# One output projection of a decoder trunk: six of eight column pairs as seven block products with GpSimd's sums, and the order of work at two borders of the attention heads

## The reference, cut to what matters

```python
def pool_mixer(h, prefix, qpos, w_in, w_grp, pool_scale, w_out):   # layer 0
    u, z = split(h @ w_in)
    pooled = windowed means of u, less u, in four groups
    y = (pooled per group @ w_grp) * pool_scale * silu(z)
    return y @ w_out            # 2048 x 2048: the projection of this case
x = x + gate(c) * mixer(rms_norm(x) * (1 + scale(c)) + shift(c))
# then shared K and V from x (w_kv), layer 1: attention in three branches with
# proj = h @ w_in_b, y = sum of gate * branch * silu(z), x + gate * (y @ w_out_b)
```

## Time and profile before

| | us |
|---|---|
| median of 3 runs | 2412.46 (2411.96 to 2413.54) |
| the profiled execution's own time | 2413.57 |
| its span, first to last instruction | 2411.8 |
| mean granted TensorE clock | 0.993 of full speed |
| first output projection, eight pairs, TensorE | 724.5 to 909.1 |
| 24 block pairs of the second input projection | to 1723 |
| heads, 8 turns | 1726 to 2120 |

### The profile page before, as it was taken

How to read it: one execution, slowest core, us unless ns; L and a number is a source line. 1 busy time by engine, 2 the same in 40 slices (tenths; PEclk the granted TensorE clock), 3 DMA queues, 4 the chain that set the end, 5 groups by cost and what they waited for, 6 DMA issues and landing times.

```text
span 2411.8 us, 48917 instructions
## 1 busy us (share of the span) xinstructions
PE 2351.8 (98%) x20327; PEld 2217.5 (92%) x20327; DVE 1178.2 (49%) x2057; ACT 824.4 (34%) x1383; POOL 348.4 (14%) x509
## 2 busy tenths in 40 slices
PE   7999999999999999999989999999999999998997
PEld 7988988888899999999989999999989988867997
DVE  1236111222163344333587777777566666654343
ACT  1125121111242233111364444444455455532222
POOL 2002000592000000110110000000032333313000
PEclk9999999999999999999999999999999999999999
DMA  9985887676644435773434444444533333497222
GB/s 341 347 294 189 272 251 246 198 226 225 218 135 146 130 110 190 227 246 108 139 92 132 132 131 131 132 131 132 158 108 104 97 97 105 158 337 281 88 88 89
DMA packets 400917, 419.69 MB, mean 174 GB/s; under 512 B 21734, under 2 KB 353766, under 8 KB 398322
## 3 DMA queue, kind: packets, MB, share of 16 engines
q1 hardware_dynamic: 384610, 349.70, 46.0%
q0 software_dynamic: 16112, 67.14, 8.2%
HBM read 383.59 MB, written 55.27 MB: 182 GB/s over the span
## 4 chain that ended last, share of the span: by engine, by line
PE 92%; DVE 4%; ACT 1%; issue 1%; DMA 1%; POOL 0%; SPq 0%; ACTq 0%; DVEq 0%; POOLq 0%
PE acc L2463 43%; PE acc L2614 19%; PE acc L2641 8%; PE work L2378 4%; PE work L2667 3%; PE work L2318 3%; PE out_acc L2704 2%; PE work L2733 1%; PE acc L2318 1%; PE acc L2689 1%; PE work L2366 1%; PE acc L2746 1%; PE out_acc L2699 1%; PE work L2658 1%; PE work L2549 1%
## 5 line engine op out<-in xcount | busy, mean ns | idle before, releaser
L2463 PE MATMUL acc<-h_hi,w_hi 128*128 128x260 f32 x2832 | 581.6, 287 | 2.5 <-DVE w_lo L1568 1.9
L1568 DVE TENSOR_TENSOR w_lo<-raw,w_hi 128x1024 fp32r<-128x1024 f32 (+1 forms) x220 | 272.4, 1239 | 624.3 <-ACT w_hi L1139 624.2
L2463 PE MATMUL acc<-h_hi,w_lo 128*128 128x260 f32 x2832 | 570.7, 283 | 0.0
L2463 PE MATMUL acc<-h_lo,w_hi 128*128 128x260 f32 x2832 | 569.8, 283 | 0.0
L1139 ACT ACTIVATE w_hi<-raw 128x1024 fp32r<-128x1024 f32 (+1 forms) x220 | 231.0, 1051 | 784.9 <-PE acc L2463 773.5
L2463 PEld LDWEIGHTS acc<-h_hi,w_hi 128*128 128x128 f32 x2832 | 436.0, 189 | 29.1 <-issue 27.7
L2463 PEld LDWEIGHTS acc<-h_hi,w_lo 128*128 128x128 f32 x2832 | 436.8, 189 | 0.0
L2463 PEld LDWEIGHTS acc<-h_lo,w_hi 128*128 128x128 f32 x2832 | 436.7, 189 | 0.0
L1901 DVE TENSOR_TENSOR block_lo<-block,block_hi 128x1024 fp32r<-128x1024 f32 x168 | 205.3, 1223 | 107.0 <-ACT block_hi L1381 106.9
L1381 ACT ACTIVATE block_hi<-block 128x1024 fp32r<-128x1024 f32 x168 | 177.6, 1057 | 191.1 <-DVE block L1936 64.4
L2614 PE MATMUL acc<-t_hi,block_hi 128*128 128x260 f32 x768 | 217.3, 283 | 3.5 <-DVE block_lo L1901 2.1
(11 more groups left out here) (415 smaller groups left out, 3485.5 us busy)
## 6 DMA issues: line engine op xcount, KB each, us to landing
ada<-in_w_ada SPq DMA_DIRECT2D x192, 512.0 KB, 4.8
block<-in_w_in_b SPq DMA_DIRECT2D x96, 512.0 KB, 4.6
raw<-in_w_in_a SPq DMA_DIRECT2D x64, 512.0 KB, 5.0
raw<-in_w_kv SPq DMA_DIRECT2D x48, 512.0 KB, 3.6
raw<-in_w_out_a SPq DMA_DIRECT2D x32, 512.0 KB, 3.8
raw<-in_w_in_b SPq DMA_DIRECT2D x32, 512.0 KB, 4.4
raw<-in_w_out_b SPq DMA_DIRECT2D x32, 512.0 KB, 3.6
pages_early<-in_cache_k_cmp SPq DMA_DIRECT2D x32, 256.0 KB, 4.2
```

The source lines that it names most:

```text
L1568: V.tensor_tensor(LO[j % 2][:, :, 0:n], RAW[j][:, :, 0:n], HI[j % 2][:, :, 0:n].bitcast(F32), ALU.subtract).then_inc(lo_ready, 1)
L2463: last = mm_(out[half][0:n, 0:HT], part[slot][:, kk, cols_], src[:, k, half * HT:(half + 1) * HT], start=(first and part is HI and src is ...
```

## The change

Pairs 0 and 7 of the output projection stay dense. Pairs 1 to 6 become seven block products each: `A_ROLE` says which of the four weight buffers a product takes, A11, A22, A12 or A21 (roles 0 to 3), or a sum that replaced it. GpSimd makes four weight sums of 128 x 1024 in each pair and, during pair 0, four activation sums of 128 x 2080 in place in Y; these are split to TH_A and TL_A by ScalarE (`t_hi_a`) and VectorE (`t_lo_a`). A product is multiplied with its high weights first (16 matmuls) and waits for the low weights only then (8 matmuls). ScalarE copies products 1 and 5 out of PSUM, VectorE reads the others (`a_out`) and adds the rows to X (`row_add`: its last operations, of 8 columns, are the sample tokens'). P7 is added by TensorE into the bank of P6 after VectorE has read that. The squares of the next norm follow the new order of rows. GpSimd's DMAs of the bias table stand between the weight sums.

In the heads, the very first scores come behind the first three pieces instead of ahead of them. `z_out` is cut in two: `z_first` (silu of the first half, which is in SBUF) signals VectorE by `csr`, and in the last turn it stands ahead of the last `turned`; `z_rest` follows. VectorE's product with the first half's z waits for `csr` and no more for the banks.

```diff
-Q_U, ..., Q_OA, Q_KV, Q_G, Q_P, Q_H, Q_OB = 0, ..., 18, 26, 38, 39, 81, 89
+Q_U, ..., Q_OA, Q_KV, Q_G, Q_P, Q_H, Q_OB = 0, ..., 18, 32, 44, 45, 87, 95
+A_PAIR, A_PROD = 6, 7
+A_P1, A_P4, A_P2, A_P5, A_P6, A_P7, A_P3 = range(A_PROD)
+A_ROLE = (0, 1, 2, 3, 3, 0, 2)
...
+        TH_A = nc.alloc_sbuf_tensor_at("y_t_hi", [P, KT, T], F32R, offset=c_at)
+        TL_A = nc.alloc_sbuf_tensor_at("y_t_lo", [P, KT, T], F32R, offset=y_at)
...
# SyncE
-            quads(Q_OA, w_oa, 8)
+            quads(Q_OA, w_oa, 1)
+            def a_load(i, role):
+                k0, c0 = ((0, 0), (8, P), (8, 0), (0, P))[role]
...
+            def a_free(i, role):
+                last = A_PROD * (i - 2)
+                if i == 1:
+                    sp.wait_ge(lo_ready, 4 * Q_OA + role + 1)
+                elif role == 1:
+                    sp.wait_ge(s_sum, 4 * (i - 2) + 3)
+                elif role == 3:
+                    sp.wait_ge(s_sum, 4 * (i - 2) + 4)
+                    sp.wait_ge(lo_ready, a_count(last + A_P6))
+                else:
+                    sp.wait_ge(lo_ready, a_count(last + (A_P7 if role == 0 else A_P3)))
+            for i in range(1, A_PAIR + 1):
+                for role in range(4) if i == 1 else (1, 3, 0, 2):
+                    a_free(i, role)
+                    a_load(i, role)
...
# GpSimd, behind the loads of x
+            b11, b12 = Y[:, 0:8, 0:HT], Y[:, 0:8, HT:T]
+            b21, b22 = Y[:, 8:KT, 0:HT], Y[:, 8:KT, HT:T]
+            pool.wait_ge(ys, 8)
+            nc.gpsimd.tensor_tensor(b11, b12, b11, ALU.subtract).then_inc(s_pooled, 1)
+            pool.wait_ge(ys, KT)
+            nc.gpsimd.tensor_tensor(b12, b22, b12, ALU.subtract).then_inc(s_pooled, 1)
+            pool.wait_ge(s_pooled, 6)
+            nc.gpsimd.tensor_tensor(b22, b22, b11, ALU.subtract).then_inc(s_pooled, 1)
+            pool.wait_ge(s_pooled, 7)
+            nc.gpsimd.tensor_tensor(b21, b22, b21, ALU.subtract).then_inc(s_pooled, 1)
...
+            for i in range(A_PAIR):
+                p = A_PROD * i
+                pool.wait_ge(raw_full[3], 16 * (Q_OA + i + 2))
+                pool.wait_ge(lo_ready, a_count(p + A_P1))
+                nc.gpsimd.tensor_tensor(a11, a11, a21, ALU.subtract).then_inc(s_sum, 1)
+                pool.wait_ge(s_sum, 4 * i + 1)
+                pool.wait_ge(raw_full[1], 16 * (Q_OA + i + 2))
+                nc.gpsimd.tensor_tensor(a21, a21, a22, ALU.add).then_inc(s_sum, 1)
+                if i < NH // 4:
+                    bias_table(i)
+                pool.wait_ge(lo_ready, a_count(p + A_P5))
+                nc.gpsimd.tensor_tensor(a21, a22, a11, ALU.subtract).then_inc(s_sum, 1)
+                pool.wait_ge(s_sum, 4 * i + 3)
+                pool.wait_ge(lo_ready, a_count(p + A_P2))
+                nc.gpsimd.tensor_tensor(a12, a12, a21, ALU.subtract).then_inc(s_sum, 1)
...
# ScalarE
+            hi(Q_OA, 1)
+            t_hi_a(0)
+            hi(Q_OA, 2)
+            t_hi_a(1)
+            t_hi_a(2)
+            hi(Q_OA, 3)
+            t_hi_a(3)
+            a_hi(0)
+            for p in range(A_PROD * A_PAIR):
...
+                    a_hi(p + 1)
...
+                if s in (A_P1, A_P5):
+                    act.wait_ge(w_used, a_count(p))
...
+                    nc.scalar.activation(copy[:, :], bank[:, 0:HT], ACT.Copy).then_inc(st_copied, 1)
+                if s in (A_P4, A_P5):
+                    square_a(2 * i + (s == A_P5))
...
                 if last_turn:
                     turned(i, 6)
+                    z_first(i)
                     turned(i, 7)
-                z_out(i)
+                else:
+                    z_first(i)
+                z_rest(i)
...
# VectorE
+            turn_a(0, {1: lambda: None, 2: lambda: t_lo_a(1), 3: lambda: t_lo_a(0), 0: lambda: (a_lo(0), t_lo_a(3))})
+            for p in range(A_PROD * A_PAIR):
...
+                    a_lo(p + 1)
...
+                if p == 0:
+                    t_lo_a(2)
+                if s in (A_P2, A_P6, A_P7, A_P3):
+                    a_out(p)
+                if s in (A_P4, A_P5):
+                    square_sum_a(2 * i + (s == A_P5))
...
+            def a_out(p):
...
+                elif s == A_P7:
+                    V.tensor_tensor(P1A[:, :], D[3][:, 0:HT], P1A[:, :], ALU.add).then_inc(st_added, 1)
+                    o(V.tensor_tensor(P5A[:, :], P5A[:, :], P1A[:, :], ALU.add))
+                    V.scalar_tensor_tensor(out=P1A[:, :], in0=D[2][:, 0:HT], scalar=-1.0, in1=P1A[:, :],
...
+                    row_add(row + 1, 1, P5A)
+                    row_add(row + 1, 0, P1A).then_inc(s_ute, 1)
+                elif s == A_P3:
+                    V.tensor_tensor(U2A[:, :], D[1][:, 0:HT], U2A[:, :], ALU.add).then_inc(st_added, 1)
...
+                    row_add(row, 1, U2A).then_inc(s_ute, 1)
...
-                if br == 2:
+                if br == 2 and hh == 0:
+                    dve.wait_ge(csr, 18 + i - back + 1)
+                elif br == 2:
                     dve.wait_ge(acc_free, 2 * (D_H + i - back) + 2)
...
# TensorE
-            pairs(Q_OA, D_OA, 8, (ys, 0))
+            for j in range(4):
+                quad(Q_OA, D_OA, j, (ys, 0))
+            def a_product(p):
...
+                elif s == A_P7:
+                    pe.wait_ge(st_added, 5 * i + 2)
...
+                out = D[(0, 2, 0, 1, 3, 3, 1)[s]]
+                k0, at = ((0, 0), (8, 0), (8, 0), (0, 0), (8, HT), (0, HT), (8, HT))[s]
+                b_hi, b_lo = (HH, HL) if s in (A_P1, A_P2, A_P3) else (TH_A, TL_A)
...
+                pe.wait_ge(hi_ready, a_count(p))
+                for kk in range(8):
+                    for part, b in enumerate((b_hi, b_lo)):
+                        mm_(out[:, 0:HT], w_hi[:, kk, :], b[:, k0 + kk, at:at + HT], ...)
+                pe.wait_ge(lo_ready, a_count(p))
+                for kk in range(8):
+                    last = mm_(out[:, 0:HT], w_lo[:, kk, :], b_hi[:, k0 + kk, at:at + HT], ...)
+                last.then_inc(w_used, a_step(p))
+            for p in range(A_PROD * A_PAIR):
+                a_product(p)
+            pe.wait_ge(st_added, A_ADD)
+            for j in range(4):
+                quad(Q_A7, D_A7, j)
...
-                    if u < 6:
+                    if u < 6 and n:
                         scores(n)
                     for at in range(steps[u], steps[u + 1]):
                         piece(i, at)
+                    if n == 0:
+                        scores(n)
```

More of the change, by code:

```diff
@@ L398, in build @@
         GD = place("gates_sample", [P, NBR])
+        RT = [place(f"resid_tmp{i}", [P, TS]) for i in range(2)]
+        assert c_at + KT * T * 4 + 2 * T * 4 <= cursor[0] - 64
         GF = nc.alloc_sbuf_tensor_at("gates_T", [48, T], F32, offset=keep_end - TS * NKV * NCMP * 4)
@@ L1322, in kv_hi @@
+            def kv_hi(k):
+                act.wait_ge(w_used, 4 * Q_A7 + k // 4 + 1)
+                if k < 14:
+                    act.wait_ge(s_ute, 4 + 2 * A_PAIR)
+                else:
+                    act.wait_ge(acc_free, 2 * D_A7 + k - 13)
                 nc.scalar.activation(HH[:, k, :], X[:, k, :], ACT.Copy, scale=vec(2, k)).then_inc(hhi_ready, 1)
-            hi(Q_OA + 7, 1)
-            squares(1, 6)
-            hi(Q_OA + 7, 2)
+            hi_a7(1)
+            for n in (12, 13):
+                square_a(n)
@@ new lines, in a_lo, with row_add @@
+            def a_lo(p):
+                dve.wait_ge(hi_ready, a_count(p))
+                V.tensor_tensor(by_cols(LO[p % 2]), by_cols(RAW[A_ROLE[p % A_PROD]]), by_cols(HI[p % 2]).bitcast(F32),
+                                ALU.subtract).then_inc(lo_ready, a_step(p))
+            def row_add(row, half, src):
+                gate = MODT[:, 2 * KT + row, :]
+                x, at = X[:, row, :], half * HT
+                n = HT if half == 0 else HT - TS
+                last = V.scalar_tensor_tensor(out=x[:, at:at + n], in0=src[:, 0:n], scalar=gate[:, 0:1], in1=x[:, at:at + n], op0=ALU.mult, op1=ALU.add)
+                if half:
+                    rt = RT[row % 2]
+                    o(V.tensor_tensor(rt[:, :], src[:, n:HT], gate[:, 1:NC], ALU.mult))
+                    last = V.tensor_tensor(x[:, TP:T], x[:, TP:T], rt[:, :], ALU.add)
+                return last
@@ L1827, in beside @@
                         kv_lo(k)
-            turn_a(7, beside)
+            turn_a(A_PAIR + 1, beside)
             lo(Q_KV, 1)
@@ L1832, in _ @@
                 kv_lo(k)
-            square_sum(1, 7)
+            for n in (14, 15):
+                square_sum_a(n)
             for k in range(14, 16):
@@ L2357, in stat @@
                 for half in range(2):
-                    last = mm_(((S if r else D)[half])[:, 0:HT], ones, (SUM if r else SUM0)[:, half * HT:(half + 1) * HT], start=True, stop=True)
+                    last = mm_(((S if r else D)[half])[:, 0:HT], ones, (SUMA if r else SUM0)[:, half * HT:(half + 1) * HT], start=True, stop=True)
                 last.then_inc(stat_done, 1)
```

257 lines of the change are left out of this document (190 added, 67 removed).

## The result

The changed kernel takes 2445.2 us (median of 4 runs, 2440.66 to 2445.9) against 2413.0 of the kernel before in the same session (2411.96 to 2417.49): ratio 1.0126, 95% interval 1.0112 to 1.014, 32 us slower. The prediction said slower, but 2424, and its range ended at 2438, so the measured time lies outside it. The profiled execution is the shortest of the four, 2440.66 us (span 2439.0), 27.1 above the one of before; readings from the trace are against that.

The account below looks back on a forecast made before the run. TensorE, busy 98% of the span, was taken as the bound. Projection +21.5, first border -3.9, last border -6.0 gave +11.6 on 2413.57: 2425.2 us, or 2424 against the median; range 2398 to 2438.

Parts of the forecast that it names:

- the two engines exclude each other: VectorE and GpSimd: each waits for the other's whole instruction when both read two SBUF operands; holds 1.76 to 4.53 us.
- Gaps in pair 0: Pair 0: activation sums delay the second quad about 3.5 us and the fourth 6.6; product 1 starts 12.5 us late.
- P4's low weights: Steady block pair: VectorE's split of P4 ends at 7.2, TensorE wants it at 4.8, so 2.5 us of waiting.
- P7: Steady block pair: P7 waits until VectorE has read P6's bank and for the drain and hand-over, 1.25 us.
- the return: Back to dense: pair 7 waits for the last product's addition, which stands behind a split, +1.6 us.
- part 2: Block pairs in steady state: waits make each 24.7 us against 23.07 dense; six take 145.8 instead of 138.4, +7.4.
- The first of the six: First block pair after pair 0: its split of P4 comes ahead of the sums' clash, so it costs 22.3 us.
- First border: First border of the heads: a piece ahead of the first scores covers the bias table's wait, -3.9 us, at least 2.5.
- Last border: Last border of the heads: z_first behind turned 6 removes the 4.24 us idle and lower clock, -6.0 us, at least 4.3.
- Quick sums: Rival: GpSimd's sums as quick as the low bound, six pairs of 23.1, total about 2412 us; chance 0.17.
- No blocking: Rival: long GpSimd sums do not block VectorE, 5.7 in pair 0, pairs of 21.2, total 2399 us; chance 0.23.
- The clock falling in the pairs: Rival: waits of 2.5 us lower TensorE's clock in the block pairs, 5 x 3 us more, 2439 us; chance 0.15.

Follow-up runs that it names:

- e13: The changed kernel with GpSimd's four bias-table transfers moved into the key and value projection, one behind every fifth row's stores; 2438.64 us in one run.
- e2: The kernel before with only the last border of the heads changed, projection left dense; 2406.87 us, ratio 0.9975 to the kernel before.
- e4: The changed kernel with each GpSimd weight sum working on one column of eight instead of 1024, nearly leaving the sums out; 2415.36 us.
- e9: The changed kernel with all four weight sums of each pair done by VectorE, GpSimd keeping activation sums and tables; 2433.66 us.
- e7: The changed kernel with P3's output step moved behind the split of P4 in VectorE's queue, same work; 2444.75 us.
- e11: The changed kernel with the four bias-table transfers moved into the second input projection, after its pairs 3, 8, 13 and 18; 2462.91 us.
- e6: The changed kernel with GpSimd's four bias-table transfers moved right behind the six block pairs, same work; 2456.14 us.
- e14: The changed kernel with all sums on VectorE, tables in key/value projection, P7's t_lo in pair 0, head 1's scores behind their piece; 2397.7 us, 0.9931 to before.

## Why the prediction was wrong

**What held.** Slower, and by the mechanism named: the two engines exclude each other, for sums of any length. A sum of 1024 columns takes 2.36 to 2.43 us behind the first pair (2.4 forecast for the subtraction), one of 2080 4.68 unblocked (4.7). The addition was forecast at 1.9 and takes about 2.4 as well (2.43 at 845.69, of which VectorE's turn between the two sums is some 0.2). Gaps in pair 0: 3.67 and 4.53 us, forecast 3.5 and 6.6. The second is shorter because TensorE came to it later: behind the first gap it ran at a granted clock of 0.50 from 736 to 738 us, and the fourth quad starts at 751.48, forecast 752.0. P1 at 758.88, forecast 760.1, is near in part by luck: the fourth quad, at a mean granted clock of 0.77, takes 7.4 us in place of 5.8, and the 2.3 us of waiting that were forecast behind it did not come. P4's low weights 2.52 late (2.5), P7 0.86 and a drain (1.25), the return 1.12 (1.6).

**The step that failed** is the one on the loads in part 2: "A11 is asked when P7 is split (some 18.5) and lands 3.8 us later, 1 us before it is needed". It is asked 19.0 after P1's start (860.98 less 841.97), lands 5 to 6 us later, 9.2 in the first pair, and P1's split stands on it. The 3.8 was a median over all loads of the stage, asked far ahead; that GpSimd's four tables stand between the sums was in the description and not in the sum. What the runs show in its place is a landing some 19 us behind the table, whenever the load is asked. e13 prices this: 161.6 - 154.6 = 7.0 us. With the tables away the pairs from the second to the fifth are 25.0 to 25.9, near the 24.7.

**"The first of the six ... costs 22.3"** failed too: 26.8 with the tables away (e13), 23.1 with the activation sums nearly left out. The activation sums delay t_lo and the splits of P2 and P5 past pair 0; the forecast let all that end with P1's start. That is 4.5 us. What is left of the 14.2 us, 2.7, is half a microsecond a pair; that it is waits a little longer than forecast and TensorE's restarts is argued, not tried.

**First border**, -3.9 forecast, about +0.4 found: the step "scores of head 1 and 24 matmuls" had no wait for that head's own table. Each head has its own, and only the first one's landing stood in the earlier trace rows. **Last border**, -6.0: the values end at 2148.62 in place of 2119.82, 34.9 of that being shift, so -6.1. The rest of the 7.6 is in the stage behind it (2150.73 to 2234.61, 83.9 us), where the DMA engines are busy for 0.9 and more of the time. It takes 83.8 to 87.5 us in the kernels with the same work there, and e2 gives 6.0 in all, so this rest is no gain of the border; why the stage varies is not explained.

**The rivals.** Quick sums: refuted by 2.4 us a sum. No blocking: refuted by 2.33 us for 8 columns, though e4 shows what it would have been, pairs of 21.2 where no table disturbs. The clock falling in the pairs: it fell to 0.94 in four of six, but not at a cost of 3 us each, since the pair of clock 1.00 takes 26.46 and its neighbours 26.62 and 26.64. The slower matmuls ran while the loop was waiting for something else. So the time passed the range's upper end by a mechanism that no rival named.

Sum: 34.5 + 0.4 - 7.6 = 27.3, of the 27.2 between the spans. The other 5 us between the medians are not in the profiled execution; the other three runs had spans of 2443.0 to 2444.1, and I have no trace of them. The stage behind the heads is near its shortest in the one that was traced, so part of the 5 may lie there; that is a guess.

## What to carry to other kernels

An order whose buffers are reloaded inside one period can make a loop through the load: close it on paper (split, load, split, and back), and take the landing from loads that stand beside the same transfers, not from a median of the stage. Here the time from the table to the landing (19 us) was fixed, so asking earlier gained nothing (e9), and the same edit at P4 cost 0.9 us a pair beside a table and gained 1.1 where there was none (e7). Look for what holds the load before shortening what stands behind it. And in this kernel the sums of weights belong on the engine that splits them: VectorE does in 1.2 us what costs both engines 2.4 when GpSimd does it.

## What the runs showed of the hardware

- One table's transfer (1 MB from DRAM to DRAM) ahead of a load of 512 KB lifts its landing from 4.6 to 13.4 us (e11), and four at once to 44 (e6). Beside dense pairs, with loads asked four quads ahead, the same transfers cost nothing (e13).
- A load that is asked while a table's transfer runs lands at a fixed time behind the table's issue: 18.7 to 19.9 us in 15 loads of four kernels, 19.8 to 21.1 in e11's four. So it lands 7.2 us behind its request when asked 11.5 us behind the table, and 11.6 when asked 8.2 behind it (both e9).
- An operation of 8 columns on VectorE is recorded with 2.3 us when it stands behind a sum of GpSimd, 0.16 without. Busy time of VectorE beside GpSimd's sums counts blocking: 114.4 us in e13 without the sums, 113.9 in e14 with all 24 of them.
